# An all-float32 transformer block: FIRST moves to 4 in two up phases, C22, S1 T1 and U change their places

## The reference, cut to what matters

```python
def swiglu_ffn(x, w_in, w_out):
    gate, up = jnp.split(x @ w_in, 2, axis=-1)
    return (jax.nn.silu(gate) * up) @ w_out

def conv_ffn(x, w_up, conv_w, conv_b, w_down):      # D_FF_2 = 2816, FFN_CONV_K = 3
    up = x @ w_up
    a, g = up[..., :D_FF_2], up[..., D_FF_2:]
    g = causal_dwconv(g, conv_w) + conv_b
    return (jax.nn.gelu(g) * a) @ w_down

def mixer_c(x, w_in, conv_w, w_out):
    proj = x @ w_in
    gate_b, gate_c, h = jnp.split(proj, 3, axis=-1)
    y = gate_b * causal_dwconv(gate_c * h, conv_w)
    return y @ w_out
```

## Time and profile before

| | |
|---|---|
| median of 3 runs | 2287.01 us |
| the profiled execution's own time | 2293.73 us |
| its span, first to last instruction | 2291.9 us |
| busy: PE, DVE, ACT, POOL | 99%, 67%, 44%, 15% |
| granted TensorE clock, mean | 0.998 |
| chain that ended last | PE 96%, DVE 2%, DMA 1% |

### The profile page before, as it was taken

How to read it: one execution, slowest core, us unless ns; L and a number is a source line. 1 busy time by engine, 2 the same in 40 slices (tenths; PEclk the granted TensorE clock), 3 DMA queues, 4 the chain that set the end, 5 groups by cost and what they waited for, 6 DMA issues and landing times.

```text
span 2291.9 us, 35530 instructions
## 1 busy us (share of the span) xinstructions
PE 2274.3 (99%) x15278; PEld 2081.8 (91%) x15278; DVE 1542.2 (67%) x1756; ACT 1019.2 (44%) x1283; POOL 354.9 (15%) x222
## 2 busy tenths in 40 slices
PE   9999999999999999999999999999999999999998
PEld 8999889897799998898988999988998988999987
DVE  7777436564587764356846999835886656999835
ACT  5555335455555543234333555522453442555521
POOL 2332000230133220001000322100230000322100
PEclk9999999999999999999999999999999999999999
DMA  4333323212133332242421333332233522232331
GB/s 171 111 111 111 110 74 139 74 52 78 37 113 109 111 111 102 74 173 90 168 90 37 129 105 112 112 115 77 108 100 124 200 74 74 93 108 99 129 109 55
DMA packets 34732, 238.83 MB, mean 104 GB/s; under 512 B 4108, under 2 KB 4492, under 8 KB 6800
## 3 DMA queue, kind: packets, MB, share of 16 engines
q1 hardware_dynamic: 34432, 236.56, 29.5%
q10 hardware_dynamic: 144, 0.00, 0.0%
HBM read 234.46 MB, written 2.10 MB: 103 GB/s over the span
## 4 chain that ended last, share of the span: by engine, by line
PE 96%; DVE 2%; DMA 1%; POOL 0%; ACT 0%; issue 0%; SPq 0%; DVEq 0%; POOLq 0%
PE bank L646 33%; PE bank L780 30%; PE bank L629 18%; PE bank L745 4%; PE bank L1132 4%; PE bank L768 1%; PE bank L986 1%; PE bank L1160 1%; PE bank L1181 1%; DVE w_lo L1871 1%; DMA raw<-w_full 1%; PE bank L918 0%; PE bank L928 0%; PE bank L825 0%; DVE s_lo L1987 0%
## 5 line engine op out<-in xcount | busy, mean ns | idle before, releaser
L1871 DVE TENSOR_TENSOR w_lo<-raw,w_hi 128x2048 fp32r<-128x2048 f32 (+1 forms) x207 | 475.1, 2296 | 362.5 <-ACT w_hi L1306 313.2
L1306 ACT ACTIVATE w_hi<-raw 128x2048 fp32r<-128x2048 f32 x207 | 395.1, 1909 | 326.0 <-DMA raw<-w_full 319.5
L780 PE MATMUL bank<-w_hi,h_hi 128*128 128x512 f32 x692 | 269.9, 390 | 0.0
L780 PE MATMUL bank<-w_hi,h_lo 128*128 128x512 f32 x692 | 269.4, 389 | 0.0
L780 PE MATMUL bank<-w_lo,h_hi 128*128 128x512 f32 x692 | 269.3, 389 | 0.0
L562 POOL TENSOR_TENSOR s_raw<-raw 128x512 f32<-128x512 f32 x84 | 115.7, 1378 | 545.0 <-PE bank L646 385.4
L646 PE MATMUL bank<-t_hi,s_hi 128*128 128x256 f32 x672 | 187.5, 279 | 3.2 <-ACT cc L1360 3.2
L646 PE MATMUL bank<-t_hi,w_hi 128*128 128x256 f32 x672 | 187.3, 279 | 3.0 <-DVE h L2023 3.0
L646 PE MATMUL bank<-u_hi,w_hi 128*128 128x256 f32 x672 | 187.5, 279 | 0.0
L646 PE MATMUL bank<-u_hi,w_lo 128*128 128x256 f32 x672 | 187.3, 279 | 0.0
L646 PE MATMUL bank<-u_lo,w_hi 128*128 128x256 f32 x672 | 187.2, 279 | 0.0
(11 more groups left out here) (386 smaller groups left out, 6096.9 us busy)
## 6 DMA issues: line engine op xcount, KB each, us to landing
raw<-w_full SPq DMA_DIRECT2D x207, 1024.0 KB, 4.9
rows_ab<-rows SPq DMA_DIRECT2D x8, 1024.0 KB, 7.0
x<-x SPq DMA_DIRECT2D x4, 512.0 KB, 4.5
mem_raw<-mem SPq DMA_DIRECT2D x2, 1024.0 KB, 9.0
out<-x SPq DMA_DIRECT2D x3, 512.0 KB, 2.6
raw<-w_full SPq DMA_DIRECT2D x2, 512.0 KB, 7.3
ab_rows<-ab_rows SPq DMA_DIRECT2D x1, 768.0 KB, 6.4
wg_raw<-w_gates SPq DMA_DIRECT2D x1, 512.0 KB, 7.2
```

The lines of the kernel that those rows point to most:

```text
L780: done = mm(bank[:, 2 * t + n, :], act_in[:, k, tok(t)], w[:, s, c0:c0 + T], start=(first and r == 0 and j == 0), stop=(last and r == 1 an ...
L1306: S.activation(w_hi[:, u % SLOTS, :], raw[:, u % SLOTS, :], ACT.Copy).then_inc(w_hi_done, 1)
L1871: V.tensor_tensor(w_lo[:, u % SLOTS, at:FULL], raw[:, u % SLOTS, at:FULL], w_hi[:, u % SLOTS, at:FULL], ALU.subtract).then_inc(w_split, 1)
```

## The change

`FIRST` becomes 4 for up2 and up3. Unit 3 there is plain, in banks 4 and 5, and unit 4 is the first seven. In all four up phases C22 of unit FIRST+1 moves forward on DVE, from behind C12 and C11 of its own unit to the end of the iteration of unit FIRST, right behind the split of unit FIRST+2; and ACT copies S1 T1 of unit FIRST+2 at the start of iteration FIRST+1. In cin, ACT copies U of unit u+1 ahead of its wait for the multiply of unit u.

```diff
-FIRST = {0: 3, 1: 3, 2: 3, "c": 4, 3: 3}
+FIRST = {0: 3, 1: 3, 2: 4, "c": 4, 3: 4}
...
         def c22_first(f, u):
-            return u == FIRST[f] or (f == "c" and u == FIRST[f] + 1)
+            return u in (FIRST[f], FIRST[f] + 1)
...
                     if n in (FIRST[f], FIRST[f] + 1):
                         copy_a11b11(f, n + 1)
-                    if n == FIRST[f]:
+                    if n in (FIRST[f], FIRST[f] + 1):
                         copy_s1t1(f, n + 1)
...
-                    if is_seven(f, n + 1) and n != FIRST[f]:
+                    if is_seven(f, n + 1) and n not in (FIRST[f], FIRST[f] + 1):
                         copy_s1t1(f, n + 1)
...
                         if u < 2:
                             high_tokens("c", u)
+                        if is_seven("c", u + 1):
+                            copy_u("c", u + 1)
                         act.wait_ge(*freed("cin", u))
                         if u < 8:
                             S.activation(yc[:, u, :], ch[:, u % 2, :], ACT.Copy,
                                          scale=vec[:, cw + 16 + u:cw + 17 + u]).then_inc(SIG["c_conv_start"], 1)
-                        if is_seven("c", u + 1):
-                            copy_u("c", u + 1)
...
                     elif is_seven(f, n):
                         c12(f, n)
                         c11(f, n)
-                        c22(f, n)
+                        if not c22_first(f, n):
+                            c22(f, n)
...
                         if n == FIRST[f]:
                             split_upto(U0[name] + n + 2)
+                            c22(f, n + 1)
```

## The result

| | before | after |
|---|---|---|
| median | 2286.82 us (4 runs, 2281.83 to 2291.79) | 2302.42 us (4 runs, 2299.86 to 2303.03) |
| ratio | | 1.0065, 95% interval 1.0039 to 1.0091 |
| the profiled execution, its span | 2293.73, 2291.9 us | 2302.01, 2300.1 us |

The change costs 15.6 us (9 to 21), or 0.65%. That is over the 0.5% which the prediction took as its bound between "same" and "slower", and the interval, 0.39% to 0.91%, does not settle on which side of it the change lies. The forecast was +9.4, which lies within the 9 to 21, and 2302.4 lies in the range. The two profiled executions differ by 8.2 us only; why is said under "two paces".

What follows compares the result with a forecast made beforehand. PE, busy 99% of the span, was taken to bound the kernel. 3.4 + 6.4 + 3.2 - 1.7 - 1.9 = +9.4 us on the shown median of 2287.0 gave 2296.4 us, range 2286 to 2306.

Steps and rivals of the forecast that it cites:

- cascade: Up2 and up3: DVE stays behind, PE waits again before unit 3, half clock follows; +16.6 us, 2303.6, chance 0.20.
- Part 1: Up2 and up3: a plain unit takes 11.20 us against a seven's 9.52, once per phase; +3.4 us.
- Part 2: Head of up2 and up3: DVE's first weight sum awaits unit 4's load, so PE waits 3.2 us before unit 2; +6.4 us.
- Part 3: Up2 and up3: PE's clock halves behind the new wait before unit 2, 1.6 us per phase; +3.2 us.
- rival with the clock kept up: Up2 and up3: no half clock follows the new waits; +6.2 us, 2293.2, chance 0.18.
- Part 5: Cin: the earlier copy of U restarts PE sooner, until it waits for C22 of unit 6; -1.9 us.
- Part 4: All four up phases: earlier C22 of unit FIRST+1 removes part of PE's waits; -1.7 us.
- theory K: Follow-up theory, not in the forecast: the new places cost some 5 us through a matmul pace that is slow more often.
- late sum: Rival, head of up2 and up3: the delayed first weight sum stays hidden from PE; -0.2 us, 2286.8, chance 0.05.
- the stalls: Rival, up phases and cin: the new places remove all of PE's waits there; +5.2 us, 2292.2, chance 0.07.

Runs made afterwards that it cites:

- e3: Changed kernel with unit 4's first weight sum (and its related sums) at the end of unit 1 in up2 and up3; +8.2 us (3.4 to 12.8) against before.
- e1: Kernel before with FIRST = 4 in up2 and up3, without the new places for C22, S1 T1 and U; +10.8 us (6.9 to 14.4).
- after again: The changed kernel, unchanged, run once more for its profile alone; span 2304.1 us.
- e2: Changed kernel with FIRST = 3 again in up2 and up3, so only C22, S1 T1 and U moved; +5.0 us (0.9 to 9.2) against before.
- e12: The kernel of e2 measured a second time; +1.8 us (-2.7 to 6.2) against the kernel before.
- e10: e2's kernel with C22 of every seven a step earlier, up phases and cin, and U of unit FIRST+2 copied before the high sums; +247 us (240 to 253).

## Why the prediction was right or wrong

The direction, the main mechanism (the load behind the first sum) and the range were right. The sum was 6 us short, with two terms mis-sized in the same direction, and the outcome that it gave 0.70, no change beyond 0.5%, is not what the medians show. That 2302.4 lies in the range is partly luck: the range reached up to 2306 for a cascade that did not come.

**Part 1** held: +3.4 forecast. The last plain unit takes 11.20 us from start to start in every profile, that of after included, and e3 has +3.7 at equal pace, though +8.2 in its timed runs.

**Part 2** held to a tenth: waits of 3.23 and 3.26 us against 3.2, by the chain as written, DVE idle 8.24 us against 8.4. The landing took 4.8 us in both phases, so the row was the one to build on. The Trainium skill's page "DMA: Bandwidth & Descriptors", section Bandwidth, gives 6.15 us for 1 MB issued by GpSimd; SP's loads in this trace were faster.

**Part 3** had the mechanism and treated it as certain, with one size. I forecast 3.2 us; the profiled execution lost 5.5, its repetition 4.2, e1 1.5: 3.7 on average. One stretch of the earlier trace rows was the whole base, and it came behind matmuls of half the width. The rival with the clock kept up was no rival but one of the draws.

**Parts 4 and 5** are the step that failed: the gains of 1.7 and 1.9 us that the new places were to bring. Part 5: forecast -1.9, measured alone +0.4. I wrote that C22 of unit 6 ends at 1684.22, since DVE's queue "is full up to there and does not get it sooner". It got it later: POOL's sum, released earlier by PE, stretched the taps before it by 0.9 us. And the half clock, 1.7 us, fell in the second wait; I had that as the lower bound of the part and left it out of the forecast, though a wait of over 2 us was what had brought it. -1.9 + 0.9 + 1.7 = +0.7. Part 4: forecast -1.7. The waits and pauses of PE in the four up phases sum to 5.1 and 5.3 us in the two profiles of before, and to 5.6, 4.8, 5.2 and 4.3 in those of after, after again, e2 and e12: 0.2 less on average. I had looked for the next late result on DVE alone. The next one was on ScalarE, whose copy of U stood behind the high sums (waits of 0.35 us in up0 and 0.41 in up2 and up3), and then its copy of S1 T1 (0.41). At equal pace all new places together gave -0.8 and -1.0, and timed +5.0 and +1.8; a gain of 3.6 is in neither.

**Sum.** At equal pace, in the profiled execution: 3.4 + 6.5 + 5.5 - 0.9 = 14.5 against 14.9 read. With the average half clock 3.4 + 6.5 + 3.7 - 0.9 = 12.7 against 15.6 timed, within its interval. The timed runs by themselves divide the loss otherwise: 10.8 for the plain units and the head (e1) and 5.0 or 1.8 for the new places (e2, e12). The 3 us between the two accounts, if they are real, are those of theory K, and stay open.

**Rivals.** No cascade: PE waits before neither unit 3 nor unit 4 of up2. The late sum was not hidden, the stalls did not go. The number came out beside the cascade's 2303.6 for other reasons.

## What to carry to other kernels

A constant like FIRST also names the slot and the load behind an operation that stands first in a queue: when it changes, look for what that engine now waits for before all else. A wait removed by moving one operation is worth only the distance to the next late operation, on every engine that feeds the same consumer, and whatever that consumer now releases earlier may slow the next one; and an operation moved ahead of its time helps only while its engine is late. Where runs of one kernel lie 10 us apart, read the pace of the matmuls in each profile before taking the difference of two spans.

## What the hardware showed

Matmuls of one shape, with the granted clock at 1.00, start every 0.1133 or every 0.1178 us; the pace holds from one stop of PE to the next and is not the same in two executions of one program. It costs 6 to 7 us for each up phase, up to some 26 us in a run by my estimate, and 30 runs of before lay between 2280.0 and 2304.5 us. The fastest of them had a span of 2278.2 us, about that of before at equal pace. So the pace is probably the bulk of the scatter, though only profiled executions show it. What chooses it was not found. The half clock behind a wait of PE is likewise not fixed by the wait: none at 0.8 to 1.1 us, and behind waits of 2.4 to 3.4 us in up2 and up3 a loss of 0, 0, 1.5, 1.5, 1.55, 2.65, 2.65 and 2.84 us; behind the wait of 2.6 to 2.75 us in cin 1.5 to 1.7 in most profiles, and none in e1 and in e2. In e10, where such a wait comes back in every unit, it followed 58 of 60.
